# Mixer tiles turned inside the retention and the state chain; small gathered experts stacked in pairs

## The reference, cut to what matters

```
scores = softmax(x @ router_w); 2 experts of 16 are chosen for each row
for e in range(16): y += combine[:, e:e+1] * ((silu(x @ w_gate[e]) * (x @ w_up[e])) @ w_down[e])
```

## Time and profile before

| | us |
|---|---|
| median of 3 runs | 2599.98 (2597.93 to 2602.13) |
| the profiled execution, its own time | 2603.51 |
| its span | 2601.7 |
| granted clock, mean | 0.972 of full speed |
| small experts (first turn of hidden rows to the last), layer 0 | 1734.0 to 1976.9 |
| small experts, layer 1 | to 2570.6 |
| state part of the mixer, layer 0 | about 313 to 424 |
| state part of the mixer, layer 1 | about 948 to 1059 |

### The profile page before, as it was taken

How to read it: one execution, slowest core, us unless ns; L and a number is a source line. 1 busy time by engine, 2 the same in 40 slices (tenths; PEclk the granted TensorE clock), 3 DMA queues, 4 the chain that set the end, 5 groups by cost and what they waited for, 6 DMA issues and landing times.

```text
span 2601.7 us, 38914 instructions
## 1 busy us (share of the span) xinstructions
PE 2431.6 (93%) x14366; PEld 1990.5 (77%) x14366; DVE 1674.4 (64%) x2114; ACT 1178.4 (45%) x1447; POOL 104.0 (4%) x82
## 2 busy tenths in 40 slices
PE   9999999999999989999999889999998897999997
PEld 8998787998998878799876778975544686976543
DVE  5665766666666675666544665668776546668776
ACT  5554423444554532344422334456664332446663
POOL 0000141000000032000000000000000000000000
PEclk9999999999999999999998999999998997999998
DMA  6667303555567620365553334678895432578884
GB/s 196 179 199 215 109 1 98 168 181 174 174 180 221 185 66 1 116 191 179 182 176 105 114 113 124 192 254 307 307 314 187 141 107 81 171 233 314 308 311 168
DMA packets 386970, 458.11 MB, mean 176 GB/s; under 512 B 18542, under 2 KB 273170, under 8 KB 386706
## 3 DMA queue, kind: packets, MB, share of 16 engines
q1 hardware_dynamic: 381824, 446.35, 54.0%
q10 hardware_dynamic: 5010, 9.98, 1.3%
HBM read 451.56 MB, written 1.05 MB: 174 GB/s over the span
## 4 chain that ended last, share of the span: by engine, by line
PE 48%; issue 36%; DVE 11%; ACT 3%; POOL 2%; SPq 0%; DMA 0%; ACTq 0%; POOLq 0%; DVEq 0%; PEldq 0%
PE PS L1952 3%; PE PS L1954 3%; PE PS L1953 3%; PE PS L2059 3%; PE PS L2061 2%; PE PS L2060 2%; DVE wlo L1793 2%; PE PS L2154 2%; PE PS L1969 2%; PE PS L1970 2%; PE PS L1971 2%; PE PS L2156 1%; PE PS L2155 1%; ACT whi L785 1%; PE PS L2078 1%
## 5 line engine op out<-in xcount | busy, mean ns | idle before, releaser
L1180 DVE TENSOR_TENSOR wlo<-raw,whi 128x1024 fp32r<-128x1024 f32 x336 | 409.7, 1223 | 299.2 <-ACT whi L738 296.2
L738 ACT ACTIVATE whi<-raw 128x1024 fp32r<-128x1024 f32 x336 | 353.6, 1055 | 360.2 <-PE PS L1954 291.5
L1952 PE MATMUL PS<-xTh,whi 128*128 128x256 f32 x1792 | 508.7, 284 | 6.5 <-DVE xTl L1147 4.7
L1954 PE MATMUL PS<-xTh,wlo 128*128 128x256 f32 x1792 | 507.8, 283 | 0.0
L1953 PE MATMUL PS<-xTl,whi 128*128 128x256 f32 x1792 | 507.7, 283 | 0.0
L1952 PEld LDWEIGHTS PS<-xTh,whi 128*128 128x128 f32 x1792 | 344.2, 192 | 12.5 <-DVE xTl L1147 5.7
L1953 PEld LDWEIGHTS PS<-xTl,whi 128*128 128x128 f32 x1792 | 344.2, 192 | 3.9
L1954 PEld LDWEIGHTS PS<-xTh,wlo 128*128 128x128 f32 x1792 | 344.3, 192 | 0.0
L1793 DVE TENSOR_TENSOR wlo<-raw,whi 128x1024 fp32r<-128x1024 f32 x188 | 222.2, 1217 | 34.6 <-ACT whi L785 34.4
L785 ACT ACTIVATE whi<-raw 128x1024 fp32r<-128x1024 f32 x188 | 190.9, 1051 | 44.3 <-PE PS L2061 15.8
L2154 PE MATMUL PS<-whi,xTh 128*128 128x416 f32 (+2 forms) x480 | 183.7, 383 | 17.7 <-DVE xTl L1147 7.5
(11 more groups left out here) (473 smaller groups left out, 4504.3 us busy)
## 6 DMA issues: line engine op xcount, KB each, us to landing
raw<-in_l_e_gate_dram SPq DMA_DIRECT2D x128, 512.0 KB, 5.1
raw<-in_l_e_up_dram SPq DMA_DIRECT2D x128, 512.0 KB, 6.0
raw<-in_l_e_down_dram SPq DMA_DIRECT2D x128, 512.0 KB, 4.9
raw<-in_ffn_w_gate_dram SPq DMA_DIRECT2D x88, 512.0 KB, 5.3
raw<-in_ffn_w_up_dram SPq DMA_DIRECT2D x88, 512.0 KB, 6.2
raw<-in_ffn_w_down_dram SPq DMA_DIRECT2D x88, 512.0 KB, 3.4
raw<-in_w_in_dram SPq DMA_DIRECT2D x64, 416.0 KB, 4.1
raw<-in_l_xkv_dram SPq DMA_DIRECT2D x32, 512.0 KB, 3.8
```

What stands on the lines that cost most here:

```text
L738: nc.scalar.activation(whi[:, m if slot is None else slot], raw[:, m, j], ACT.Copy).then_inc(hi_done[m], 1)
L1180: nc.vector.tensor_tensor(wlo[:, w], raw[:, m, j], whi[:, w].bitcast(F32), ALU.subtract).then_inc(lo_done[m], 1)
L1952: mm(out_, whi[:, m, ks], xTh[:, k, :], start=(k == 0), stop=False)
L1954: last = mm(out_, wlo[:, m, ks], xTh[:, k, :], start=False, stop=(k == KB - 1))
```

## The change

**Experts.** Slots 4 to 11 (at most 64 rows) are stacked in pairs (4,5), (6,7), (8,9), (10,11): `BLOCK` gives 9 blocks for 13 slots, `ROW_AT` the first row (0 or 64). The turned hidden tile of a paired slot is 128 columns wide for each of four parts, with zeros where the other slot is (`turn_e` first fills the PSUM bank with a product of zeros); `hidden_e` copies 512 columns; `down_e` of both slots adds into the same two banks; `out_e` and `scatter` run only for the last slot of a block (0, 1, 2, 3, 5, 7, 9, 11, 12). `pickT` has 9 blocks; its rows from 64 on are made by a plain product with the identity, after a zero fill of two banks. In ACT's and DVE's order one split moves ahead of `out_e`.

**Mixer.** The values of the retention go to banks 4 and 5. The transposes of t = 0 stand before `values(2)`, those of t = 1 in the state chain of t = 0 in place of two `warm` groups (`turn_keys(1)` in chunk 0, `turn_queries(1)` in chunk 1), into banks 4 to 7; the ACT copy has a second buffer. The third `warm(3)` before them is gone. Level 0 of the solve turns `Aoff` by a transpose in place of a product, and DVE does its `TT` tile before `TM`. DVE's side work moves behind the second addition of a level (`beside`); the bonus moves from before the loop to there (levels 3 and 4 of t = 0), its first product behind the copies of t = 0.

The core of the diff:

```
+ALONE = sum(c > 64 for c in CAPS)
+BLOCK = tuple(i if i < ALONE else ALONE + (i - ALONE) // 2 for i in range(NR))
+NB = BLOCK[-1] + 1
+ROW_AT = tuple(64 * (i >= ALONE and (i - ALONE) % 2) for i in range(NR))
+LAST_OF = tuple(max(i for i in range(NR) if BLOCK[i] == b) for b in range(NB))
+ROWS = tuple(ROW_AT[i] + CAPS[i] for i in LAST_OF)
+WIDTH = tuple(P if BLOCK.count(BLOCK[i]) > 1 else CAPS[i] for i in range(NR))
...
-        ART = RA[:, 4096:5120].rearrange("p (q n) -> p q n", q=4)
+        ARTs = [RA[:, 4096:5120].rearrange("p (q n) -> p q n", q=4), gain[:, 0].rearrange("p (q n) -> p q n", q=4)]
...
                                 silu_e(0)
                             hidden_e(i - 1)
                             split_e()
+                            split_e()
                             if i > 1:
                                 out_e(i - 2)
-                        for _ in range(5 if i else 6):
+                        for _ in range(4 if i else 6):
                             split_e()
...
+                def copy_turned(t):
+
+                    act.wait_ge(tr_psum, 2 * l + t + 1)
+                    nc.scalar.activation(ARTs[t].rearrange("p q n -> p (q n)"), PS[:, 4 * t:4 * t + 2, :].rearrange("p b n -> p (b n)"),
+                                         ACT.Copy).then_inc(tr_copied, 1)
+
+                copy_turned(0)
                 act.wait_ge(ret_o, l + 1)
-                nc.scalar.activation(xn[:, :, RW:2 * RW], PS[:, 0:2, :], ACT.Copy).then_inc(ret_oc, 1)
+                nc.scalar.activation(xn[:, :, RW:2 * RW], PS[:, 4:6, :], ACT.Copy).then_inc(ret_oc, 1)
                 for t in range(NT):
-                    act.wait_ge(tr_psum, 2 * l + t + 1)
...
+                    else:
+                        copy_turned(1)
...
-                own(TTop(tmp, r_, av, ALU.mult))
-                own(TTop(tmp, tmp, row(par[:, 4]), ALU.mult))
-                own(nc.vector.tensor_reduce(bonus[:], tmp.rearrange("p t (h n) -> p (t h) n", h=RH), AX.X, ALU.add))
...
+                def beside(t, lev):
+
+                    if t == 0 and lev == 1:
+                        dve.wait_ge(ret_oc, l + 1)
+                        own(TTop(sq, o, o, ALU.mult))
+                    if t == 0 and lev == 2:
+                        own(nc.vector.tensor_reduce(rs_in[:, 0:8], sq.rearrange("p t (h n) -> p (t h) n", h=RETH), AX.X, ALU.add))
+                        nc.vector.tensor_scalar(rs_in[:, 0:8], rs_in[:, 0:8], 1.0 / 128, 1e-6, ALU.mult, ALU.add).then_inc(rs_asked, 1)
+                    if t == 0 and lev == 3:
+                        own(TTop(kk, kk, row(par[:, 4]), ALU.mult))
+                    if t == 0 and lev == 4:
+                        own(nc.vector.tensor_reduce(bonus[:].rearrange("p (t h) -> p t h", t=NT), heads(kk), AX.X, ALU.add))
+                    if t == 1 and lev == 1:
+                        head_mean(0)
+                    if t == 1 and lev == 2:
+                        head_var(0)
+
                 for t in range(NT):
                     dve.wait_ge(tr_psum, 2 * l + t + 1)
-                    if t:
+                    nc.vector.tensor_copy(BT.rearrange("p q n -> p (q n)"), PS[:, 4 * t + 2, :])
+                    nc.vector.tensor_copy(KT.rearrange("p q n -> p (q n)"), PS[:, 4 * t + 3, :]).then_inc(tr_copied, 1)
+                    if t == 0:
+
+                        own(TTop(kk, r_, av, ALU.mult))
+                    else:
                         dve.wait_ge(y_psum, 2 * l + t)
-                    nc.vector.tensor_copy(BT.rearrange("p q n -> p (q n)"), PS[:, 2, :])
-                    nc.vector.tensor_copy(KT.rearrange("p q n -> p (q n)"), PS[:, 3, :]).then_inc(tr_copied, 1)
                     for h in range(RH):
                         dve.wait_ge(L_psum, 16 * l + 8 * t + h + 1)
-                        TTop(Lm[:, h], PS[:, 4 + h % 4, :], lmask, ALU.mult).then_inc(L_ready, 1)
+                        TTop(Lm[:, h], PS[:, ret_bank(h), :], lmask, ALU.mult).then_inc(L_ready, 1)
...
+                                dve.wait_ge(aoff_ready, base + 1)
+                                TTop(TT[:, hs], Aoff[0][:, hs], idb, ALU.add)
                                 dve.wait_ge(q_psum, base + 1)
-                                dve.wait_ge(aoff_ready, base + 1)
-                                TTop(TM[:, hs], PS[:, 2 + hf, :].rearrange("p (h n) -> p h n", h=4), idb, ALU.add)
-                                TTop(TT[:, hs], Aoff[0][:, hs], idb, ALU.add).then_inc(t_ready, 1)
+                                TTop(TM[:, hs], PS[:, 2 + hf, :].rearrange("p (h n) -> p h n", h=4), idb, ALU.add).then_inc(t_ready, 1)
...
+                            if hf:
+                                beside(t, lev)
...
+                for b in range(ALONE // 2, NB // 2):
+                    mm(PS[:, TURN_BANKS[b], :], zero[:, 0:P], zero[:], start=True, stop=True)
...
                     for t in range(NT):
-                        c0 = i % 2 * S + t * P
-                        last = nc.tensor.transpose(PS[0:CAPS[i], TURN_BANKS[i // 2], c0:c0 + P], pick[:, t, SLOT_AT[i]:SLOT_AT[i + 1]].bitcast(F32), ident)
-                    if i % 2 or i == NR - 1:
+                        c0 = b % 2 * S + t * P
+                        out_, of = PS[r0:r0 + CAPS[i], TURN_BANKS[b // 2], c0:c0 + P], pick[:, t, SLOT_AT[i]:SLOT_AT[i + 1]].bitcast(F32)
+                        last = mm(out_, of, ident, start=True, stop=True) if r0 else nc.tensor.transpose(out_, of, ident)
+                    if i == LAST_OF[b] and (b % 2 or b == NB - 1):
...
-                    C = CAPS[i]
+                    C, opens = WIDTH[i], not ROW_AT[i]
                     pe.wait_ge(eT_lo, NR * l + i + 1)
-                    if i:
-                        pe.wait_ge(eo_lo, NR * l + i)
+                    if i and opens:
+                        pe.wait_ge(eo_lo, NB * l + BLOCK[i])
...
+                    if WIDTH[i] > C:
+                        mm(PS[:, GB, :], zero[:, 0:P], zero[:], start=True, stop=True)
                     for f in range(4):
-                        last = nc.tensor.transpose(PS[:, GB, f * C:(f + 1) * C], hrows[0:C, f * P:(f + 1) * P], ident[0:C, 0:C])
+                        at_f = f * WIDTH[i] + c0
+                        last = nc.tensor.transpose(PS[:, GB, at_f:at_f + C], hrows[0:C, f * P:(f + 1) * P], ident[0:C, 0:C])
...
-                    pe.wait_ge(eo_lo, NR * l + i + 1)
+                    pe.wait_ge(eo_lo, NB * l + blk + 1)
                     for t in range(NT):
                         for b in range(2):
-                            to = pickT[0:C, i, t * P:(t + 1) * P]
-                            mm(PS[:, 2 * t + b, :], to, outh[0:C, b * 512:(b + 1) * 512], start=False, stop=False, skip_group_check=True)
-                            last = mm(PS[:, 2 * t + b, :], to, outl[0:C, b * 512:(b + 1) * 512], start=False, stop=False, skip_group_check=True)
+                            to = pickT[0:R, blk, t * P:(t + 1) * P]
+                            mm(PS[:, 2 * t + b, :], to, outh[0:R, b * 512:(b + 1) * 512], start=False, stop=False, skip_group_check=True)
+                            last = mm(PS[:, 2 * t + b, :], to, outl[0:R, b * 512:(b + 1) * 512], start=False, stop=False, skip_group_check=True)
...
+                    o = [PS[:, 4 + t, h * P:(h + 1) * P] for t in range(NT)]
...
+                def turn_keys(t):
+
+                    for q in range(4):
+                        qs = slice(q * P, (q + 1) * P)
+                        nc.tensor.transpose(PS[:, 4 * t + 2, qs], tl[:, 1, t, qs], ident)
...
+
                 scores(3)
+                pe.wait_ge(tilde, l + 1)
+                turn_keys(0)
+                turn_queries(0)
                 values(2)
                 values(3).then_inc(ret_o, 1)
-                pe.wait_ge(ret_oc, l + 1)
...
-                    if t:
-
-                        warm(3)
-                        pe.wait_ge(y_ready, 2 * l + t)
-                        pe.wait_ge(z_state, 3 * l + 2)
...
+                        if t == 0 and h == 2:
+                            pe.wait_ge(ret_oc, l + 1)
...
+                                last = mm(out_, Aoff[lev % 2][:, h], TM[:, h], start=True, stop=True) if lev else nc.tensor.transpose(out_, Aoff[0][:, h], ident)
...
+                    if t:
+
+                        pe.wait_ge(y_ready, 2 * l + t)
...
+                        elif ch == 1:
+                            turn_queries(1)
...
+                        if ch:
+                            warm(3, 0)
+                        else:
+                            turn_keys(1)
```

More of the change, by code:

```diff
@@ L1430, in _ @@
                                     nc.vector.tensor_copy(TT[:, 4 * b:4 * b + 4].rearrange("p h n -> p (h n)"), PS[:, 6 + b, :]).then_inc(tt_ready, 1)
-                            if t == 0 and hf == 0 and lev == 2:
-                                own(nc.vector.tensor_reduce(rs_in[:, 0:8], sq.rearrange("p t (h n) -> p (t h) n", h=RETH), AX.X, ALU.add))
```

(12 more changed lines are left out.)

71 lines of the change are left out of this document (36 added, 35 removed).

## The result

The changed kernel took 2557.2 us, median of 4 runs (2553.39 to 2564.19), beside 2598.95 (4 runs, 2591.54 to 2602.13) for the kernel before. The ratio is 0.9848, with a 95% interval of 0.9831 to 0.9864: 39.5 us less, between 35 and 44. The forecast was 2560 (2549 to 2579), from 40.1 us less.

What follows compares the result with a forecast made beforehand. TensorE, busy 93% of the span, was taken as the bound. Experts 25.8 less 5 for turning `pick` plus mixer 19.3 gave 40.1 us off 2603.5, so 2563.4; set against the median, 2560, range 2549 to 2579.

Steps and rivals of the forecast that it cites:

- The late split: Experts: `out_e` behind one more split readies w3l 1.2 us earlier; 11 x 0.79 = 8.7 us saved per layer.
- Four scatters: Experts: four of thirteen scatters go, 2.15 us each, nothing hides them; 8.6 us saved per layer.
- Fill and wide tiles: Experts' turn, 8 paired slots: zero fill loses 1.8 us, wider hidden tile 2.6 us by stall at chunk 3, per layer.
- Loads: Experts: 12 chunks per shorter period need 328 GB/s, at worst 348; no stall taken.
- Rival (a): Experts: loads bind, taking nearly all of the 25.8 us; 2584 us, chance 0.10.
- (b): Experts' down product: weight loads of 128 columns are exposed, 23 us; 2583 us, chance 0.05.
- Turning the selection matrix: Turning `pick`: plain products and two zero fills add 2.5 us per layer, nearer to half clock; 5 us lost.
- End of the retention: Mixer: transposes right after the scores start L earlier, 3.6 us in layer 0, 2.6 in layer 1; 6.2 together.
- a low granted clock between 310 and 420: Mixer, profile after: one of the signs named as making the prediction wrong.
- Second half: Mixer: L of t = 1 starts right behind y's products, 4.1 us earlier per layer, 8.2 in all.
- The solve: Mixer: moved side work and quicker level 0 save 1.05 (t = 0) and 1.4 us (t = 1), 4.9 for two layers.
- Rival (c): Mixer's solve: moved side work and GpSimd lock each other longer, losing 8 us, no gain; 2573 us, chance 0.08.

Runs made afterwards that it cites:

- the swapped kernel: Changed kernel with each pair's first slot on rows 64 on, the second on rows 0 on, narrow tile, no zero fill in the turn: 2545.44 us.
- the new order alone: Kernel before with only one split moved ahead of `out_e` on ScalarE and VectorE, no pairs: 2579.59 us, ratio 0.9924.
- the mixer's part alone: Kernel before with all the mixer edits of the change, experts as before: 2578.05 us, ratio 0.9918.
- experiment 3: Changed kernel with squares (t = 0) and mean (t = 1) put back before level 1's additions: 2552.56 us, ratio 0.9811 to the kernel before.
- eighth kernel: Changed kernel with each pair's first slot on rows 64 on, no zero fill in the turn, and VectorE's side work spread: 2538.16 us, ratio 0.9774 to before.

## Why the prediction was right, step by step

**The late split** (8.7 for each layer): shown. Alone it gave 8.9, 0.8 in each iteration as the rows had it, and nothing took its place; the low part of the down result came in time.

**Four scatters** (8.6) and more: a period without scatter lasts 17.5 in the swapped kernel, one with it 19.65 under the new order alone, so 2.15 each for those that are gone. The ones that stay are 0.2 shorter as well (1.86 in place of 2.05), which I had not seen, though the kernel before has it: its scatters of 76 to 104 rows last 1.86, and only those of 64 rows and fewer 2.05. The 12.9 for each layer came out as 14.85: 8.6 + 0.8 (shorter scatters) + 8.9 - 1.7 - 1.75.

**Fill and wide tiles** (1.8 + 2.6): the fill was 1.73, measured by doubling it. The swapped pairs give 3.5 for all of it, so 1.75 is left for the wide copies and the wide stationary tiles, where I had 2.6. The wait at chunk 3 came, at 0.13 to 0.18 in place of 0.33.

**Loads** (no stall): right, 335 GB/s over four periods. Rival (a) did not occur, and neither did (b): the down products with 128 columns start 0.23 apart (1858.98 to 1859.21).

**Turning the selection matrix** (2.5 lost for each layer): from the last small product to the gather passed 5.16 us on the mean of six stages in kernels with the old code (4.25 to 5.59) and 6.88 on the mean of fourteen with the new (6.43 to 7.88). So 1.7 was lost; I had taken a price near half clock, and the granted clock was 0.78 over the stage in most of the fourteen.

**End of the retention** (6.2 in all): 3.4 for each layer at full clock, where I had 3.6, and 4.3 at 0.65, where I had 2.6 against a layer at 0.72. In the two profiled executions it shows as 1.85 only, since layer 0 had full clock before and half clock after. The forecast of L at 313.1 was therefore off in the profile and right in the kernel. What I named as a thing that would make me wrong, a low granted clock between 310 and 420, was there for some 4 us; the mixer's part alone has the same code at full clock, so it is no sign against the change.

**Second half** (4.1 for each layer): 4.05.

**The solve** (2.45 gained for each layer) is the step that failed. Measured: 0.48 lost for t = 0 and 0.04 gained for t = 1. I had written that behind the second addition an operation of 1.22 is nearly free and that the squares cost 0.8. The runs show what is free: about 1.1 us, the 0.59 in which VectorE is idle and what TensorE can bear. What is longer delays the next level by the rest. Take a piece's length from its own start to the start of the copy behind it, and 4.74 as the level without side work (4.71 for level 4):

| piece of side work | its length | what the level lost | forecast |
|---|---|---|---|
| squares, t = 0 | 2.33 | 1.24 | 0.8 |
| sum with its second step, t = 0 | 1.72 | 0.56 | 0 |
| bonus product, t = 0 | 1.25 | 0.13 | 0 |
| mean, t = 1 | 3.04 | 1.93 | 1.6 |
| variance, t = 1 | 1.75 | 0.60 | 0 |

Length less loss is 1.1 to 1.2 in every row. I had priced this slack at some 1.5, and had counted the sum and the variance as free. Level 0 failed too: levels 0 and 1 together gained 0.45 in t = 0 (7.45 to 7.00) and 1.22 in t = 1 (8.22 to 7.00), where I had 0.8 and 1.6. The sign that I had named, level 2 near 4.9 us, did not come, and one that would make me wrong did: the moved side work delays the levels, 2 and 3 above all. It was too small to carry the whole forecast with it.

Rival (c) came half true: the solve gave nothing, but it lost 0.9 in all and not 8. Squares of this form take 1.22 without GpSimd at work, so 1.08 of the 2.30 goes by the timeline to GpSimd's masks, two of which run from 328.38 to 330.88; an experiment that takes the masks away was not made. The Trainium skill (SBUF — State Buffer, Who interferes with whom) says that an instruction of VectorE with two SBUF inputs and one of GpSimd that reads SBUF exclude each other; by that rule the squares are held wherever a mask is running, in the old place as in the new. They were: 2.29 and 2.30, and 1.69 in experiment 3.

**The sum.** By stages: 29.7 (experts) - 3.4 (turning) + 8.1 (second half) - 0.9 (solve) = 33.5, and the retention adds 6.8 (both layers at full clock) to 8.7 (both at 0.65): 40.3 to 42.2. The runs say 38.6 at one clock and 39.5 by the ratio. That the forecast's 40.1 came so close is partly luck: the experts gave 3.9 more and the turning cost 1.6 less than forecast, and the solve gave 5.8 less.

## What to carry to other kernels

Look first for the split or copy that stands in program order in front of one that the bound engine waits for: moving it by one place gave half of this change's gain. Side work in a serial chain is free up to a measured slack and costs its excess above that, so cut it into pieces shorter than the slack and put long ones where the engine is idle. When two profiled executions are compared, compare stage by stage at the same granted clock, or fit the time of many runs against their clock, before a difference of 5 us is given a cause.

## What the runs showed of the hardware

- The granted clock differs from one execution of a kernel to the next, 0.969 to 0.980 on the mean, and each 0.001 was worth 2.17 us. The end of the retention, with the same instructions, ran at full clock in some executions and for some 10 us at 1.2 GHz in others, at a price of 4.5 us. Why one execution falls and another doesn't, no run here shows.
- Products of 64 rows or fewer between products of 128 rows cost a little more. At the scatters of 36 to 64 rows in the kernel before (slots 4 to 10, full clock) three distances are 0.31 to 0.34 in place of 0.23: before the first product, before the second, and before the first of 128 rows again (with 56 rows 1860.94 to 1861.27, 1861.27 to 1861.61 and 1863.00 to 1863.32). Such a scatter lasts 2.05. At those of 76, 88 and 104 rows there are none, 0.23 to 0.24 throughout, and a scatter lasts 1.85 to 1.87 (with 76 rows 1820.53 to 1822.39), like that of 120 rows in the changed kernel. Between 64 and 76 rows nothing was measured.
- A small TENSOR_SCALAR of VectorE (128x8, one SBUF tensor) took 0.17 us by itself and 1.16 when it was issued while GpSimd's mask ran, and it ended with the mask. Timelines of VectorE and GpSimd, eighth kernel, level 1 of t = 1, and VectorE in level 4:

```profile
372.74 2.49 POOL L713 TENSOR_TENSOR solve_b<-RA,tab 128x512 f32<-128x512 f32 x2
372.88 1.16 DVE L1470 TENSOR_SCALAR rs_in<-rs_in 128x8 f32<-128x8 f32 x1
...
391.46 0.17 DVE L1436 TENSOR_SCALAR rs_in<-rs_in 128x8 f32<-128x8 f32 x1
```

The row at 372.74 holds two masks, 2.49 us together; one by itself takes 1.27, so the first ends about 374.0, and the small instruction at 374.04. It is so in every trace: in all 52 places of the eleven traces where such an instruction was issued during a mask, it ended 0.03 us after a mask; the other 80 took 0.16 to 0.17. The second steps in the solve of the changed kernel are among the 52 (0.40 to 0.55 us, as at 336.83). The Trainium skill (SBUF — State Buffer, Who interferes with whom) exempts a VectorE instruction with at most one SBUF input outside the two-port modes, and names `tensor_scalar` among those that can enter these modes and then contend with GpSimd. The 52 places agree with the second; they show that even one of 8 columns is held until the mask ends.
